# Two mixers' last four output tiles, the norm behind them and the next MLP's first four tiles, computed over 256 tokens at a time

## The reference, cut to what matters

```python
for i in range(DEPTH):                       # DEPTH = 2
    h = rmsnorm(x, g_mix_pre[i])
    if i % 2 == 0: m = conformer_conv(h, ...)      # ends in  y @ pw2_w + pw2_b
    else:          m = forgetting_attention(h, ...) # ends in  o @ w_o
    x = x + rmsnorm(m, g_mix_post[i])              # the norm behind the mixer
    h = rmsnorm(x, g_ffn_pre[i])
    x = x + rmsnorm(square(relu(h @ w_up)) @ w_down, g_ffn_post[i])
```

## Time and profile before

| | us |
|---|---|
| median of 3 runs | 1260.48 (1260.47 to 1261.01) |
| the profiled execution | 1263.37 |
| its span, first to last instruction | 1261.6 |
| PE busy | 1196.0 |
| DVE busy | 946.5 |
| ACT busy | 664.2 |
| POOL busy | 92.6 |

### The profile page before, as it was taken

How to read it: one execution, slowest core, us unless ns; L and a number is a source line. 1 busy time by engine, 2 the same in 40 slices (tenths; PEclk the granted TensorE clock), 3 DMA queues, 4 the chain that set the end, 5 groups by cost and what they waited for, 6 DMA issues and landing times.

```text
span 1261.6 us, 16041 instructions
## 1 busy us (share of the span) xinstructions
PE 1196.0 (95%) x5598; PEld 983.9 (78%) x5598; DVE 946.5 (75%) x1367; ACT 664.2 (53%) x1128; POOL 92.6 (7%) x105
## 2 busy tenths in 40 slices
PE   5899999999999999998879999999999999999996
PEld 4788888877888888886857777777878888888875
DVE  5599997479758579589577777775589569587698
ACT  4665666446544344445476666664456444353453
POOL 4000010030000000001410000000030000000000
PEclk9999999999999999999879999999999999999998
DMA  6122112511421512413011111121420521515201
GB/s 177 31 67 55 46 34 68 167 34 67 145 94 33 197 68 82 152 34 84 18 50 51 50 50 50 50 91 43 143 92 34 171 97 44 185 38 168 101 17 67
DMA packets 105625, 102.25 MB, mean 81 GB/s; under 512 B 4527, under 2 KB 88495, under 8 KB 105564
## 3 DMA queue, kind: packets, MB, share of 16 engines
q1 hardware_dynamic: 105564, 101.45, 25.3%
HBM read 99.34 MB, written 2.10 MB: 80 GB/s over the span
## 4 chain that ended last, share of the span: by engine, by line
PE 76%; DVE 12%; issue 5%; ACT 4%; POOL 1%; DMA 1%; DVEq 0%; SPq 0%; ACTq 0%; POOLq 0%
PE psum L488 14%; PE psum L490 14%; PE psum L489 14%; PE psum L663 7%; PE psum L664 7%; PE psum L665 7%; DVE hlo L1311 2%; PE psum L602 2%; PE psum L600 2%; PE psum L601 2%; DVE prob L1862 2%; PE psum L840 1%; DVE wlo L1305 1%; DVE xT L1496 1%; PE psum L499 1%
## 5 line engine op out<-in xcount | busy, mean ns | idle before, releaser
L488 PE MATMUL psum<-hhi,whi 128*128 128x512 f32 x872 | 349.5, 401 | 7.1 <-DVE wlo L1294 4.8
L490 PE MATMUL psum<-hhi,wlo 128*128 128x512 f32 x872 | 341.7, 392 | 0.0
L489 PE MATMUL psum<-hlo,whi 128*128 128x512 f32 x872 | 341.3, 391 | 0.0
L914 ACT ACTIVATE whi<-mraw 128x1024 fp32r<-128x1024 f32 x176 | 185.4, 1055 | 146.4 <-PE psum L665 136.5
L1305 DVE TENSOR_TENSOR wlo<-mraw,whi 128x1024 fp32r<-128x1024 f32 x176 | 213.3, 1221 | 47.2 <-ACT whi L914 46.8
L488 PEld LDWEIGHTS psum<-hhi,whi 128*128 128x128 f32 x872 | 165.2, 189 | 44.4 <-issue 6.6
L490 PEld LDWEIGHTS psum<-hhi,wlo 128*128 128x128 f32 x872 | 164.5, 189 | 35.4
L489 PEld LDWEIGHTS psum<-hlo,whi 128*128 128x128 f32 x872 | 165.1, 189 | 32.8 <-issue 1.0
L663 PE MATMUL psum<-whi,aop_hi 128*128 128x512 f32 x448 | 175.3, 391 | 1.9 <-DVE acc L1580 1.9
L665 PE MATMUL psum<-whi,aop_lo 128*128 128x512 f32 x448 | 174.4, 389 | 0.0
L664 PE MATMUL psum<-wlo,aop_hi 128*128 128x512 f32 x448 | 174.4, 389 | 0.0
(11 more groups left out here) (200 smaller groups left out, 1734.9 us busy)
## 6 DMA issues: line engine op xcount, KB each, us to landing
mraw<-in_mlp_w_up SPq DMA_DIRECT2D x64, 512.0 KB, 4.9
mraw<-in_mlp_w_down SPq DMA_DIRECT2D x64, 512.0 KB, 4.7
wraw<-in_conv_pw_w SPq DMA_DIRECT2D x24, 512.0 KB, 4.8
wraw<-in_attn_w_in SPq DMA_DIRECT2D x16, 512.0 KB, 4.5
wraw<-in_attn_w_in SPq DMA_DIRECT2D x16, 256.0 KB, 3.2
wraw<-in_attn_w_o SPq DMA_DIRECT2D x8, 512.0 KB, 4.0
xin<-in_x SPq DMA_DIRECT2D x4, 512.0 KB, 9.7
out_x<-xtok SPq DMA_DIRECT2D x4, 512.0 KB, 2.6
```

The lines of the kernel that those rows point to most:

```text
L488: pe.matmul(o, whi[:, u, kb, :], xhi, start=start, stop=False)
L489: pe.matmul(o, whi[:, u, kb, :], xlo, start=False, stop=False)
L490: return pe.matmul(o, wlo[:, u, kb, :], xhi, start=False, stop=stop)
L914: a.activation(split_unit(whi, e), raw_unit(c, e_), ACT.Copy).then_inc(s["m_hi"], 1)
```

## The change

At both places the 512 tokens are cut in two halves: `HALF[0]` is tokens 256 to 511, `HALF[1]` is tokens 0 to 255, and the later tokens go first. The mixer's last four tiles are done for the first half and then for the second, two tiles in one psum bank (`mixer_halves`). The norm behind the mixer is done for each half by itself: `post_columns` and `post_broadcast` replace `post_stat`, and stand in PE's queue between other matmuls; the `keep_warm` calls there go. DVE, ACT and POOL do everything at the boundary on 128 x 256, first half first (`x_half`, `half_lo`, `half_hi`, `half_square`, `add_half_squares`), mixed by hand with the preparation of the MLP's weights (`m_hi`, `m_lo`) and the mixer's second half (`mixer_pair`, `add_pair`). The MLP's first four tiles follow in `first_halves`. The same halves were already in use between the two layers. The core of the diff, left-aligned by eight columns (`half_hi` and `half_square`, not shown, are lines 926 and 920 of before on 256 tokens):

```diff
+HALF = (slice(2 * P, S), slice(0, 2 * P))
+MIX_BANK = ((4, 5), (7, 4))
+POST_BANK = (6, 5)
...
+    def add_half_squares(v):
+        for rows, sq_sem, sum_sem, base in ((HALF[0], "p1_sq", "p1_sum", KB * (v // 2)),
+                                            (HALF[1], "p_sq", "p_sum", KB * v)):
+            for k in range(KB):
+                pool.wait_ge(s[sq_sem], base + k + 1)
+                sq = tmp[:, 2 + k % 2, rows]
+                if k == 0:
+                    g.tensor_copy(sumsq[:, rows], sq).then_inc(s[sum_sem], 1)
+                else:
+                    pool.wait_ge(s[sum_sem], base + k)
+                    g.tensor_tensor(sumsq[:, rows], sumsq[:, rows], sq, ALU.add).then_inc(s[sum_sem], 1)
...
-    def post_stat(b):
-        keep_warm(WARM_SQ)
-        pe.wait_ge(s["m_sum"], 7 * MIX[b] + 9)
-        columns(sumsq, True, False)
-        pe.wait_ge(s["m_sq"], KB * (MIX[b] + 1))
-        columns(tmp[:, 3, :], False, True).then_inc(s["stat"], 1)
-        keep_warm(WARM_ROOT)
-        broadcast(NTH[ST_POST[b]])
-        keep_warm(WARM_NORM)
...
+    def post_columns(l, h):
+        bank, tiles = POST_BANK[h], ((2, 3), (0, 1))[h]
+        pe.wait_ge(s["m_sum"], 12 * l + 8 + 4 * h)
+        for q in tiles:
+            mm = pe.matmul(psum[:, bank, q:q + 1], sumsq[:, q * P:(q + 1) * P], ones[:, 0:1],
+                           start=q == tiles[0], stop=True, skip_group_check=True)
+        mm.then_inc(s["stat" if h else "stat1"], 1)
+    def post_broadcast(b, h):
+        if h:
+            pe.wait_ge(s["spread"], NTH[ST_POST[b]])
+        else:
+            pe.wait_ge(s["spread1"], MIX[b] + 1)
+        pe.matmul(psum[:, POST_BANK[h], HALF[h]], ones[:, :], tmp[:, 0, HALF[h]], start=True,
+                  stop=True).then_inc(s["bcast" if h else "bcast1"], 1)
+    def mixer_halves(b, n, xh, xl):
+        l = MIX[b]
+        for h in range(2):
+            for u in range(4):
+                if h == 0:
+                    weights(n, u)
+                if h == 1 and u == 2:
+                    pe.wait_ge(s["m_done"], 12 * l + 6)
+                o = psum[:, MIX_BANK[h][u // 2], (u % 2) * 2 * P:(u % 2 + 1) * 2 * P]
+                for kb in range(KB):
+                    if h == 1 and (u, kb) == (0, 6):
+                        post_columns(l, 0)
+                    if h == 1 and (u, kb) == (1, 4):
+                        post_broadcast(b, 0)
+                    hi, lo = xh[:, kb, HALF[h]], xl[:, kb, HALF[h]]
+                    pe.matmul(o, whi[:, u, kb, :], hi, start=u % 2 == 0 and kb == 0, stop=False,
+                              skip_group_check=True)
+                    pe.matmul(o, whi[:, u, kb, :], lo, start=False, stop=False, skip_group_check=True)
+                    mm = pe.matmul(o, wlo[:, u, kb, :], hi, start=False, stop=u % 2 == 1 and kb == KB - 1,
+                                   skip_group_check=True)
+                if h == 1:
+                    mm.then_inc(unit[u // 2], 1)
+                elif u % 2:
+                    mm.then_inc(s["m_pair"], 1)
+    def half_product(bank, hi, lo, h, kb):
+        o, xh, xl = psum[:, bank, HALF[h]], hhi[:, kb, HALF[h]], hlo[:, kb, HALF[h]]
+        pe.matmul(o, hi, xh, start=h == 0 and kb == 0, stop=False, skip_group_check=True)
+        pe.matmul(o, hi, xl, start=False, stop=False, skip_group_check=True)
+        return pe.matmul(o, lo, xh, start=False, stop=kb == KB - 1, skip_group_check=True)
+    def half_unit(u, h, kb):
+        return half_product(u, whi[:, u, kb, :], wlo[:, u, kb, :], h, kb)
+    def first_halves(l, v, b, pairs=4):
+        for r in range(2):
+            pe.wait_ge(s["m_ready"], MLP_UNITS * l + 2 * r + 2)
+            for kb in range(pairs):
+                if (r, kb) == (1, 2):
+                    post_columns(l, 1)
+                pe.wait_ge(s["h1_ready"], KB * (v - 1) + kb + 1)
+                for u in (2 * r, 2 * r + 1):
+                    half_unit(u, 0, kb)
+        for kb in range(pairs, KB):
+            if kb == pairs + 1:
+                post_broadcast(b, 1)
+            pe.wait_ge(s["h1_ready"], KB * (v - 1) + kb + 1)
+            for u in range(4):
+                half_unit(u, 0, kb)
+        for kb in range(KB - 2):
+            pe.wait_ge(s["h_ready"], KB * v + kb + 1)
+            for u in range(4):
+                half_unit(u, 1, kb)
+        pe.wait_ge(s["h_ready"], KB * v + KB)
+        for u in range(4):
+            for kb in (KB - 2, KB - 1):
+                mm = half_unit(u, 1, kb)
+            mm.then_inc(s["m_unit"], 1)
+            if u == 1:
+                pe.wait_ge(s["p1_sum"], KB * (v // 2 + 1))
+                pre_columns(v)
+            if u == 2:
+                broadcast(NTH[ST_PRE[v]])
...
     first_step(N_PW2, s["c_ready"], 0)
-    for u in range(4):
-        pe.wait_ge(s["m_done"], u + 3)
-        whole_unit(N_PW2 + 1, u)
-    post_stat(0)
+    mixer_halves(0, N_PW2 + 1, hhi, hlo)
...
-        first_step(None, s["h_ready"], KB * v, v, l=l)
+        first_halves(l, v, 2 * l)
...
+    def mixer_pair(b, dst, bias_row, h, g):
+        bank = MIX_BANK[h][g]
+        if bias_row is None:
+            a.activation(post_sq[:, h, g, :], psum[:, bank, :], ACT.Square).then_inc(s["m_sq"], 1)
+            a.activation(dst[:, 4 + 2 * g:6 + 2 * g, HALF[h]],
+                         psum[:, bank, :].rearrange("p (a b) -> p a b", b=2 * P),
+                         ACT.Copy).then_inc(s["m_done"], 2)
+            return
         for i in range(2):
-            for u in range(4):
-                k = 4 * i + u
-                done(n0 + i, u)
-                if bias_row is None:
-                    e = a.activation(dst[:, k, :], psum[:, u, :], ACT.Copy)
-                else:
-                    e = a.activation(dst[:, k, :], psum[:, u, :], ACT.Identity,
-                                     bias=vcol(bias_row, k))
-                e.then_inc(s["m_done"], 1)
-                square(dst[:, k, :], k, s["m_done"], KB * MIX[b] + k + 3, s["m_sum"],
-                       7 * MIX[b] + k + 1, s["m_sq"])
-                if i == 0:
-                    split_hi(n0 + 1, u)
-                elif u < 3:
-                    m_hi(MIX[b], u)
-        root(ST_POST[b])
-        m_hi(MIX[b], 3)
+            cols = slice(i * 2 * P, (i + 1) * 2 * P)
+            q = a.activation(post_sq[:, h, g, cols], psum[:, bank, cols], ACT.Square,
+                             bias=vcol(bias_row, 4 + 2 * g + i))
+        q.then_inc(s["m_sq"], 1)
+        for i in range(2):
+            cols = slice(i * 2 * P, (i + 1) * 2 * P)
+            a.activation(dst[:, 4 + 2 * g + i, HALF[h]], psum[:, bank, cols], ACT.Identity,
+                         bias=vcol(bias_row, 4 + 2 * g + i)).then_inc(s["m_done"], 1)
+    def mixer_norm(n0, b, dst, bias_row, v, row):
+        l = MIX[b]
+        def both(h, k):
+            half_hi(v, row, h, k)
+            half_square(v, h, k)
+        act.wait_ge(s["stat1"], l + 1)
+        a.activation(rms[:, 2:4], psum[:, POST_BANK[0], 2:4], ACT.Sqrt, scale=1.0 / D,
+                     bias=eps[:, 0:1]).then_inc(s["root1"], 1)
+        m_hi(l, 0)
+        both(0, 0)
+        done(n0 + 1, 1)
+        mixer_pair(b, dst, bias_row, 1, 0)
+        m_hi(l, 1)
+        both(0, 1)
+        both(0, 2)
+        m_hi(l, 2)
+        both(0, 3)
+        done(n0 + 1, 3)
+        mixer_pair(b, dst, bias_row, 1, 1)
+        m_hi(l, 3)
+        act.wait_ge(s["stat"], NTH[ST_POST[b]] - (NTH[ST_POST[b]] > NTH[ST_VAR]))
+        a.activation(rms[:, 0:2], psum[:, POST_BANK[1], 0:2], ACT.Sqrt, scale=1.0 / D,
+                     bias=eps[:, 0:1]).then_inc(s["root"], 1)
+        for k in range(4, KB):
+            both(0, k)
+        for k in range(KB):
+            both(1, k)
...
+    def add_pair(l, h, g):
+        dve.wait_ge(s["m_sq"], 8 * l + 5 + 2 * h + g)
         for i in range(2):
-            for u in range(4):
-                k = 4 * i + u
-                if k < KB - 1:
-                    add_square(k, s["m_sq"], KB * MIX[b] + k + 1, s["m_sum"], 7 * MIX[b] + k + 2)
-                if i == 0:
-                    split_lo(n0 + 1, u)
-                elif u < 3:
-                    m_lo(MIX[b], u)
+            dve.wait_ge(s["m_sum"], 12 * l + 4 + 4 * h + 2 * g + i)
+            d.tensor_tensor(sumsq[:, HALF[h]], sumsq[:, HALF[h]],
+                            post_sq[:, h, g, i * 2 * P:(i + 1) * 2 * P], ALU.add).then_inc(s["m_sum"], 1)
...
+    def x_half(l, row, h, k, src):
+        at_ = tmp[:, k % 2, HALF[h]]
+        x_sem, base = s["x_done" if h else "x1_done"], 2 * KB * l
+        if base + k >= 2:
+            dve.wait_ge(x_sem, base + k - 1)
+        d.scalar_tensor_tensor(at_, src[:, k, HALF[h]], vcol(row, k), psum[:, POST_BANK[h], HALF[h]],
+                               ALU.mult, ALU.mult).then_inc(s["t1_done"], 1)
+        dve.wait_ge(s["t1_done"], KB * (2 * l + h) + k + 1)
+        d.tensor_tensor(xT[:, k, HALF[h]], xT[:, k, HALF[h]], at_, ALU.add).then_inc(x_sem, 1)
...
```

(48 more changed lines are left out.)

126 lines of the change are left out of this document (73 added, 53 removed).

## The result

| kernel | median of the runs, us | lowest to highest | profiled execution: time, span |
|---|---|---|---|
| before, beside it | 1261.01 | 1260.47 to 1262.84 | 1263.37, 1261.6 |
| changed | 1270.09 | 1268.16 to 1272.91 | 1272.27, 1270.4 |

The changed kernel is slower: ratio 1.0073, 95% interval 1.0055 to 1.0092. The forecast was 1270.1. From here on "place" means what the prediction calls so: the stretch from the start of the mixer's last four tiles to tile 4 of the MLP. The "later half" is tokens 256 to 511, which are done first, the "earlier half" tokens 0 to 255.

What follows compares the result with a forecast made beforehand. PE and DVE were both taken as the bound at the boundary. Places +4.5 and +3.9 us, together +8.4, plus 1.2 for the clock gave +9.6: 1270.1 us against the median 1260.48; range 1265 to 1274, with rivals 1259.5 to 1276.

Steps and rivals of the forecast that it cites:

- The gap: PE between mixer and MLP, filled by `keep_warm`: the change removes 8.86 us behind the first mixer.
- the narrow matmuls: PE, last mixer and first MLP tiles: 192 wide matmuls become 384 narrow ones, +2.4 us a place.
- the inserts: Columns and half broadcasts inserted in PE's queue, two of each: +2.0 us a place.
- The first wait: PE ahead of the MLP's first matmul, for `m_lo` 1: 2.9 us, 0.5 shorter behind the second mixer.
- The second wait: PE behind the MLP's first two tiles, for `m_lo` 3: 2.9 us.
- the walk: Queue-by-queue timing of DVE, ACT and PE through a place: tile 4 +4.5 us at the first mixer, +3.9 at the second.
- The columns behind 12 matmuls: PE's columns for the mixer's second half finish at 266.7; root and `hhi` of block 4 follow, DVE continues at 267.5.
- POOL: Half-width POOL additions beside DVE at the boundary: each costs DVE 0.3 us, 12 of them 3.5 us.
- The clock: Half clock behind some of PE's waits: +0.6 us a place, +1.2 in all, bounds 0 and +6.
- Rival B: POOL's additions at the boundary cost nothing: tile 4 +1.0 and +0.4 us, 1261.9 us; chance 0.14.
- Rival A: DVE and ACT stay ahead of PE, gap saved: place 52.6 us, 3.1 less, 1254.3 us; chance 0.13.
- Rival C: Clock falls at each place and stays low into the tail: 3 us more each, +14.4, 1274.9 us; chance 0.18.

Runs made afterwards that it cites:

- one move on ACT: Changed kernel with the second `hhi` block and its square moved ahead of the evacuations of the earlier half's first mixer pair on ACT; 1267.15 us, ratio 1.0049.
- the first order: Changed kernel, same instructions reordered: ACT's `hhi` earlier, DVE's x blocks and first additions ahead, PE's columns and broadcast earlier; 1256.06 us, ratio 0.9960 to before.

## Why the prediction was right, point by point

- **The gap, the narrow matmuls, the inserts.** Right. The gap is gone, and narrow matmuls cost +1.26 us in a mixer where 96 x 0.013 = 1.2 were taken. The inserts can be read in the trace of the changed kernel. From the start of the columns, or of a broadcast, to the second matmul behind it, less 0.12 for the one between (not shown), they cost 0.45 and 0.43 us, where 0.5 each were taken: 1.8 in a place, not 2.0.

```profile
244.35 0.50 PE L578 MATMUL psum<-ones,sumsq 128*128 128x1 f32 x4
...
244.92 0.28 PE L608 MATMUL psum<-hlo,whi 128*128 128x256 f32 x1
...
246.95 0.59 PE L587 MATMUL psum<-tmp,ones 128*128 128x256 f32 x2
...
247.50 0.28 PE L608 MATMUL psum<-hlo,whi 128*128 128x256 f32 x1
```

- **The first wait.** Right in size and cause. On the clock of before (1.14 us later) PE came to it at 255.86 and left it at 258.52; 255.8 and 258.7 were forecast. In the second place it was 2.17, and 2.4 forecast. DVE's wait for `hhi` behind four evacuations and `m_hi` is there, and one move on ACT took 1.7 us of the wait away.
- **The second wait.** Right in the first place (2.75, and 2.9 forecast). In the second it is 1.24, for a reason that the walk had only half: the clock fell behind the first wait there (0.50 from 915.3 to 918.7), the 24 matmuls between took 1.49 us longer (start of the first to start of the last: 4.34 against 2.85), and `wlo` did not come sooner or later by it. What the clock took, the wait gave back: from the matmul behind the first wait to the one behind the second 5.87 us pass in the first place and 5.86 in the second. The two together are 2.7, the size that was forecast.
- **The columns behind 12 matmuls.** The step was in the walk (root, then `hhi` of block 4), and it holds. But I read DVE's queue behind it as the bound, and in my first expectation I drew the wrong conclusion that PE's clock would be hidden there. It is not: DVE waited 3.42 us for this chain, and moving the columns alone gave 2.8 and 1.9 us.
- **POOL.** 0.3 us was taken for each addition, 0.35 is what it costs where DVE never stops. Without the additions the places lose 3.3 and 1.6 us, by estimate 2.6 and 2.8 without the clock's part, where 3.5 each (12 x 0.3 is 3.6), plus 1.1 in the first wait, were put down. The price of one addition was right; not all of it reached the end.
- **The clock.** A term of 0.6 a place was a mean. It was 1.46 in the first place, as the prediction priced the case in which it hits the matmuls ahead of the columns with 1.1, and in the second about 0.4, by the tail (pre-norm columns to tile 4 in 5.73 us, with the broadcast at half speed, against 5.30 in the first), and 0.4 more behind tile 4. Together 2.3 against 1.2.
- **The sum.** The places grew by 5.6 and 4.0, 9.6 in all, as forecast (8.4 and 1.2). That the median agrees to 0.01 us with the 1270.1 forecast is luck: the interval of the ratio alone reaches from 7 to 12 us, the ratio itself says 9.2, and in the sum a clock term that was 1.1 us too small stands against inserts, first waits and POOL that were each taken somewhat too dear. The pre-norm columns came 55.96 and 54.00 us behind the start, where 54.9 was named.
- **Rival B** had the right sign of effect and the wrong price: without POOL the time was 1265.1, not 1261.9. It left the second wait (still 2.70) and the slow matmuls ahead of the columns out.
- **Rival A** was wrong of this kernel and right of its work. "It decides when DVE has `m_lo` 1 done by 255.8 and `m_lo` 3 by 258.7": the first order has `m_lo` 1 and 2 done by 257.4 and `m_lo` 3 by 260.5 (on the clock of before, where each time is 1.76 us later than in its own trace), later than A asked but with the columns and one short wait of PE in between, and its places are 53.3 us, where A said 52.6, its time 1256.1, where A said 1254.3. What I had called two engines at their bound was a bound only for DVE's order of that moment.
- **Rival C**, the half clock into the tail, happened in the second place only, from 946.0 to 949.5. The clock did fall in each place, once in the first and twice in the second, but in the first it was back at full level at 266.8, long before the tail.

Left open: where the clock falls in the executions that were not traced. Each kernel has one trace, and the medians of two kernels hold a share of it that the places do not show.

## What to carry to other kernels

When a stage is cut in two so that its first part overlaps the stage ahead, the queues of all engines have to be written anew: here the same instructions gave 1270.1 or 1256.1 us by their order alone, and before the change 1261. Look for the small instruction with a long chain behind it (here the column sums of two token tiles on PE, on which a root, four `hhi` and DVE's whole second half wait) and put it ahead of everything that PE could also do later. A collision, a slow clock or a long queue has no price of its own: ask which engine is late at that moment, and measure it in the order that will be kept. And before two single traces are compared place by place, look at the granted clock in both: here it moved a place by as much as the move under test.

## What the runs showed of the hardware that I had not expected

A lower clock can be free. Of two waits of the same kind, 2.75 us in the first place and 2.17 in the second, both were followed by a granted clock of 0.50, from 263.4 to 266.8 and from 915.3 to 918.7. In the first place it stood ahead of the columns and cost 1.46 us; in the second it was over before the next wait ended and cost nothing (5.87 and 5.86 us between the waits' ends). The clock did not fall behind the first place's first wait of 2.66 us: the window shows 1.00. With the columns moved, the first place has the same wait (2.64 us), and there the clock did fall. The changed kernel first, then the one with the columns moved:

```profile
257.40:260.40 3.00, 3.00 (x24) 2.91 (x24) 2.35 (x6) 2.18 (x7) 0.74 (x1) 1.00 0.64 213
```

```profile
257.54:260.40 2.86, 2.86 (x13) 2.86 (x14) 2.21 (x6) 2.03 (x6) 0.73 (x1) 0.50 0.59 158
```

13 matmuls stand there instead of 24, and this too was free: the columns come 5.86 us behind the end of the first wait, because PE then waits 0.37 us for `wlo` and not 2.75.

So the length of the wait alone does not say whether the clock falls, and of several such waits in a forecast each needs its own "if it falls here, who is late".
